# Low parts of the expert weights written over the raw chunk in a one-core MoE decoder step

## What is computed

```python
x = x + mixer(rmsnorm(x))                      # pooling and gating mixer, then w_out
h = rmsnorm(x)
top_w, top_idx = softmax_of_top4(h @ w_router + b_router)       # 32 experts
for each (token, expert) pair, in blocks of up to 128 rows of one expert:
    gu = h[rows] @ w_up[e] + b_up[e]           # w_up[e]: 1024 x 2048
    glu, lin = min(gu[:, :1024], 7), clip(gu[:, 1024:], -7, 7)
    y = (glu * sigmoid(1.702 * glu) * (lin + 1)) @ w_down[e] + b_down[e]    # 1024 x 1024
x = x + sum of the four y of a row, weighted by top_w
x = x + sigmoid(x @ w_ple_gate) * (p @ w_ple_proj)
return rmsnorm(x), and some state rows
```

## Time and profile before

| what | us |
|---|---|
| median of 3 runs | 1451.01 |
| lowest and highest run | 1450.70, 1453.27 |
| the profiled execution's own time | 1450.99 |
| its span in the trace, first to last instruction | 1448.8 |

### The profile page before, as it was taken

How to read it: one execution, slowest core, us unless ns; L and a number is a source line. 1 busy time by engine, 2 the same in 40 slices (tenths; PEclk the granted TensorE clock), 3 DMA queues, 4 the chain that set the end, 5 groups by cost and what they waited for, 6 DMA issues and landing times.

```text
span 1448.8 us, 19378 instructions
## 1 busy us (share of the span) xinstructions
PE 1407.6 (97%) x6542; PEld 1133.9 (78%) x6542; DVE 1231.5 (85%) x994; ACT 928.0 (64%) x632; POOL 210.7 (15%) x130
## 2 busy tenths in 40 slices
PE   6999988999999999999999999999999999999997
PEld 5895456888888888888888888888888888888665
DVE  5732367999999999999999999999999999999885
ACT  4311144777777777777777777777777777777522
POOL 3131000011111111111111111111111111111100
PEclk9999988999999999999999999999999999999999
DMA  7114245999999999999999999999999999999661
GB/s 259 59 62 158 88 163 213 355 375 375 376 372 372 373 372 365 374 361 369 369 372 372 367 370 373 371 369 375 371 380 368 372 376 372 373 371 364 202 239 58
DMA packets 94168, 457.31 MB, mean 316 GB/s; under 512 B 13314, under 2 KB 14894, under 8 KB 60213
## 3 DMA queue, kind: packets, MB, share of 16 engines
q1 hardware_dynamic: 84255, 437.50, 79.6%
q0 software_dynamic: 9360, 17.85, 3.2%
q10 hardware_dynamic: 526, 1.60, 0.4%
HBM read 451.76 MB, written 21.58 MB: 327 GB/s over the span
## 4 chain that ended last, share of the span: by engine, by line
PE 91%; DVE 4%; issue 1%; DMA 1%; ACT 1%; SPq 0%; POOL 0%; POOLq 0%; DVEq 0%; ACTq 0%
PE ps L1257 47%; PE ps L1266 24%; PE ps L1134 5%; PE ps L1404 2%; PE ps L1273 2%; PE ps L1245 2%; PE ps L1238 2%; DVE w_lo L1653 1%; PE ps L1070 1%; PE ps L1072 1%; PE ps L1077 1%; DMA w_v_sb<-in_w_in_dram 1%; DVE resid L1884 1%; PE ps L1149 1%; PE ps L1205 1%
## 5 line engine op out<-in xcount | busy, mean ns | idle before, releaser
L1653 DVE TENSOR_TENSOR w_lo<-raw,w_hi 128x2048 fp32r<-128x2048 f32 x384 | 867.5, 2286 | 60.6 <-PE ps L1266 60.4
L850 ACT ACTIVATE w_hi<-raw 128x2048 fp32r<-128x2048 f32 x384 | 732.4, 1916 | 215.4 <-PE ps L1257 178.0
L1257 PE MATMUL ps<-w_hi,xT_hi 128*128 128x512 f32 x1024 | 278.5, 394 | 0.0
L1266 PE MATMUL ps<-w_lo,xT_hi 128*128 128x512 f32 x1024 | 275.2, 391 | 2.7 <-DVE w_lo L1653 2.6
L1257 PE MATMUL ps<-w_hi,xT_lo 128*128 128x512 f32 x1024 | 276.1, 392 | 0.1
L1266 PEld LDWEIGHTS ps<-w_lo,xT_hi 128*128 128x128 f32 x1024 | 192.5, 188 | 44.1 <-DVE w_lo L1653 4.3
L1257 PEld LDWEIGHTS ps<-w_hi,xT_lo 128*128 128x128 f32 x1024 | 193.2, 189 | 41.9 <-DVE xT_lo L1710 0.5
L1257 PEld LDWEIGHTS ps<-w_hi,xT_hi 128*128 128x128 f32 x1024 | 190.3, 189 | 38.2 <-ACT xT_hi L873 0.2
L702 POOL DMA_INDIRECT expert_rows<-y_rows,scatter_col x32 | 138.1, 4316 | 404.5 <-ACT y_rows L887 404.5
L1257 PE MATMUL ps<-w_hi,aT_hi 128*128 128x512 f32 x512 | 140.0, 395 | 0.0
L1257 PE MATMUL ps<-w_hi,aT_lo 128*128 128x512 f32 x512 | 136.9, 389 | 0.0
(11 more groups left out here) (272 smaller groups left out, 1191.4 us busy)
## 6 DMA issues: line engine op xcount, KB each, us to landing
raw<-in_w_up_dram SPq DMA_DIRECT2D x256, 1024.0 KB, 6.6
raw<-in_w_down_dram SPq DMA_DIRECT2D x128, 1024.0 KB, 7.6
raw<-in_w_ple_gate_dram SPq DMA_DIRECT2D x4, 1024.0 KB, 5.5
yk<-expert_rows SPq DMA_DIRECT2D x4, 1024.0 KB, 8.6
raw<-expert_rows SPq DMA_DIRECT2D x4, 1024.0 KB, 7.9
resid<-in_x_prompt_dram SPq DMA_DIRECT2D x4, 512.0 KB, 10.2
w_v_sb<-in_w_in_dram SPq DMA_DIRECT2D x2, 1024.0 KB, 9.4
w_z_sb<-in_w_in_dram SPq DMA_DIRECT2D x2, 1024.0 KB, 12.7
```

What stands on the lines that cost most here:

```text
L850: act.activation(w_hi[:, s % SPLIT, :], raw[:, s % RING, :], ACT.Copy).then_inc(s_hi, 1)
L1257: mm = pe.matmul(out[:, c:c + 512], (xh, xl)[xs], w_hi[:, s % SPLIT, base + c:base + c + 512], start=(fresh and xs == 0 and base == 0), st ...
L1266: mm = pe.matmul(out[:, c:c + 512], xh, w_lo[:, s % SPLIT, base + c:base + c + 512], start=False, stop=last and k == len(parts) - 1, skip_ ...
L1653: dve.tensor_tensor(w_lo[:, s % SPLIT, :], raw[:, s % RING, :], w_hi[:, s % SPLIT, :].bitcast(F32), ALU.subtract).then_inc(s_lo, 1)
```

## The change

`w_lo` no longer has a buffer of its own: it is laid over `raw`, slot by slot, so the low part of a chunk is written over the raw chunk that it was made from. The three old slots stay allocated as `spare`, so that nothing else moves. VectorE drops its wait for the low products of chunk n - 3. A raw slot is now read last by TensorE's low products, so the loads wait for `s_lused` in place of `s_lo`; that includes the four copies of the gate's weights.

```diff
@@ buffers @@
         with ExitStack() as s:
             raw = sb("raw", [P, RING, 2 * FF], scope=s)
+        with ExitStack() as s:
+            w_lo = sb("w_lo", [P, RING, 2 * FF], F32R, scope=s)
...
-            w_lo = sb("w_lo", [P, SPLIT, 2 * FF], F32R, scope=s)
+            sb("spare", [P, SPLIT, 2 * FF], scope=s)
@@ waits @@
+        def wait_lo_used(eng, J, s):
+            eng.wait_ge(s_lused, STEP_CHUNKS * J + s + 1)
+
@@ sync: raw_free @@
                     if STEP_CHUNKS * J + s >= RING:
-                        wait_lo(sp, J, s - RING)
+                        wait_lo_used(sp, J, s - RING)
                     return
                 lo = sp.to_reg(J * STEP_CHUNKS + (s - RING + 1))
-                sp.wait_ge(s_lo, lo)
+                sp.wait_ge(s_lused, lo)
@@ tensor: lo_products @@
-                        mm = pe.matmul(out[:, c:c + 512], xh, w_lo[:, s % SPLIT, base + c:base + c + 512],
+                        mm = pe.matmul(out[:, c:c + 512], xh, w_lo[:, s % RING, base + c:base + c + 512],
@@ vector: lo_part @@
-                wait_split_used(dve, s_lused, J, s)
                 wait_hi(dve, J, s)
-                dve.tensor_tensor(w_lo[:, s % SPLIT, :], raw[:, s % RING, :], w_hi[:, s % SPLIT, :].bitcast(F32),
+                dve.tensor_tensor(w_lo[:, s % RING, :], raw[:, s % RING, :], w_hi[:, s % SPLIT, :].bitcast(F32),
                                   ALU.subtract).then_inc(s_lo, 1)
```

## The result

The change made the kernel slower by 0.3%: median 1456.68 us of 20 runs (1451.55 to 1459.74), against 1452.20 of 20 runs of the kernel before (1450.37 to 1453.63). The ratio is 1.003, interval 1.0022 to 1.0038. The forecast was 1452.0, and its range ended at 1455.2. A second set, run with the last experiments, gave 1454.46 (12 runs, 1451.90 to 1459.79) against 1452.65, ratio 1.0018 [1.0008, 1.0029]. The loss is some 0.2 to 0.4%, and a run of the changed kernel varies by 8 us where one of before varies by 3 to 4.

A forecast was written before the change was run, and what follows sets the result against it. The prediction took TensorE, busy 97% of the span, to bound the kernel. From 1450.99 us, with 0 for steps, removed wait, in-place writing and start, and +1.0 for the tail, it forecast 1452.0 us, range 1450.3 to 1455.2.

The forecast's parts named there:

- The steady steps: later by 5 us, and it fits: Expert steps: loads issue 5.2 us later, may take 8.52 us to land, worst landing estimated at 7.0; cost 0.
- Raw loads alone no longer queue: Expert steps: releases 2.72 us apart, against 2.50 us for a load's bytes, leave no queue of raw loads.
- Its lead absorbs that: Expert steps: ScalarE's high part starting at 831.2 instead of 830.82 is covered by ScalarE's lead.
- Cost: 0: Expert steps: later loads cost TensorE nothing, hidden by the four chunks it still has to work off.
- the tail: Behind the last expert: gate copy 2 lands later and delays ScalarE's last copy-out; +1.0 us, bounds 0.4 to 2.0.
- writing in place: VectorE's low parts: estimated from line 1902's in-place products at 2.31 us against 2.286, at most 0.4 per step; taken as 0.
- the removed VectorE wait: Expert steps: VectorE's 58.1 us of waiting for TensorE goes, but no product starts earlier; gain 0.
- the start: First ring load, chunk 6: lands at 223.8, its high part 0.4 us late against a lead of 4.2; cost 0.
- shorter median landings (near 5 to 6 us): Raw loads in the expert steps: a sign named in advance for the forecast being right; down loads' median before was 7.6.
- Late loads stall each step: Rival, loads sharing the DMA with the scatter: landings don't shrink, 9 us over 30 steps, so 1461; chance 0.14.
- VectorE freed: Rival, TensorE's gaps at the start: freed of a wait, VectorE removes up to 4.3 us, so 1447.7; chance 0.07.
- Nothing on the path changes: Rival, tail: copy 2 lands in 4.3 us or less, or the late copy-out is caught up; 1451.0, chance 0.17.

The follow-up runs named there:

- product_one_later: The changed kernel, with each load waiting for the low products of one chunk later: 1539.67 us, ratio 1.0575 to the kernel before.
- light scatter: The changed kernel, with the scatter of expert rows cut by its bound to row 0 and those rows filled once early: one execution, 1453.07 us.
- after_copy_out_first: The changed kernel, with the last copy-out moved ahead of the gate's third high part on ScalarE: 1456.78 us, ratio 1.0025 to the kernel before.
- low_part_one_later: The kernel before, own low-part buffer kept, each load waiting for the low part of one chunk later: 1452.21 us, ratio 0.9997.
- before_no_branch: The kernel before, with the branch over the unused overflow blocks left out of TensorE's program: 1452.42 us, ratio 0.9998.
- after_rotated_copy_first: The changed kernel, third down chunk's low products moved to the next step's head and last copy-out put first: 1454.80 us, ratio 1.0012 to the kernel before.

## Why the prediction was wrong

**Failed: "The steady steps: later by 5 us, and it fits".** The allowed 8.52 us fits the runs: with the slowest up load at 8.2 almost no lead is left, and product_one_later, which takes 2.72 from it, stalls at once. The other side was mis-sized. I took the lone landing, added the bytes of gather and scatter at the full rate, and called 7.0 us the worst. It is the median (6.9 and 7.1); the worst are 8.2 and 8.8. The step under it, "Raw loads alone no longer queue", fell: with releases at TensorE's pace, 320 of 351 loads leave with two or more others on their way, and landings stay at 7 us. The step took a spacing of 2.72 us against 2.50 for the bytes as enough, but that works off only 0.2 us of queue with each load. That no step stalled for long is luck in part: the shortest lead left is 0.05 us. I also set aside the DMA share of 0.99 because another stretch moved 420 GB/s. It was the better sign; the light scatter points to one reason, a scatter that costs more than its bytes. The Trainium skill, "DMA: Bandwidth & Descriptors" (Anatomy of one DMA), fits a DMA on the software path as 2.0 us plus the bytes at 436 GB/s, an estimate of 4.4 us for 1 MB. That is further still from what a load of this stream takes on SyncE's hardware queue, 6.9 to 7.1 us.

**Failed: "Its lead absorbs that", with the "Cost: 0" of the steps taken for the last step too.** For 29 steps it nearly does, +1.4 us in the profile, most of it in three steps. But I costed ScalarE's lateness in the steady step only, where TensorE has later work queued. I did not follow VectorE, which stands behind ScalarE, into the last step: there a branch waits behind its low part, and in the profiled execution 1.6 us of lateness became 5.4 us, by a longer branch and the fall of the clock. The row of the branch (5.13 us) and the gap it already left (1.67 us, "issue") were in the trace of before, and I read neither.

**Right in place, half in size: the tail.** +1.0 was forecast, +0.5 measured: the issue came 0.04 us behind its release, not 0.18, and the landing took 5.09, not 5.4. after_copy_out_first shows the mechanism, and that taking it out does not show in the time.

**Right:** writing in place, 0 forecast and 1 ns measured; the removed VectorE wait, worth nothing; the start, 39.95 us before and 40.10 after for the first step; SyncE's and ScalarE's new waits. The sign "shorter median landings (near 5 to 6 us)", which I had named for being right, did not appear. "No low part is written in place now" was wrong, at no cost: `gate_lo` lies over `raw`, and line 1852 writes each of the gate's low parts over its own raw slot. Its rows in the trace of before have the very shape, and show in place what line 1653 takes there into another buffer (median 2283 ns), so the detour over line 1902 was not needed:

```profile
L1852 DVE TENSOR_TENSOR gate_lo<-raw,gate_hi x4: 2273/2283/2286, 1361.7 to 1370.8; 128x2048 fp32r<-128x2048 f32 x4
```

**The rivals.** *Late loads stall each step* had the right premise, that landings do not shrink, and the right sign, but not the right place: the slowest landing was 8.8, the steps nearly held, and the loss came at the exit and in a few steps, and not 30 times. *VectorE freed* did not happen. *Nothing on the path changes* is excluded by the interval.

**What stays open:** how much of the queue in which a load takes 7 us, against 4.7 alone, is the scatter's doing; and what decides from run to run how late chunk 378 is (30.6 to 32.4 us into the last step in the traces of the changed kernel and its variants with the same release), how long the branch's packet takes to start, and whether the clock falls. That these three together make the wide spread is argued from a few traces, not shown.

## What to carry to other kernels

When a slot's release moves behind a later reader, budget the landing that loads have in the running stream, not the lone landing plus bytes: moving the issue by 5 us here left the 7 us unchanged. Then look past the steady step to the iteration behind which no further work is queued, and at any branch there: lateness that the next iteration hides is paid where the pipeline drains, and a fall of the clock can make it dearer. A wait off the path is slack: VectorE's 58 us of waiting for TensorE showed that it ran ahead, and the change turned that into waiting for landings.

## What the runs showed of the hardware

- One taken branch behind a long loop took 3.6 to 6.5 us of TensorE's sequencer: 3.61 in low_part_one_later, 5.13 in the kernel before, 6.45 in product_one_later. In all twelve traces it ended 1.3 to 1.5 us behind one 16 KB packet of an instruction queue, which started 0.95 to 4.02 us into the branch.
- Loads of 1 MB that were issued 2.7 us apart landed 2.5 to 2.6 us apart in the changed kernel, so that a queue shrank by 0.2 us a load and landings stayed near 7 us.
- Whether the clock falls is not told by the length of the gap alone. It fell at the exit behind gaps of 4.27, 4.19, 3.30 and 2.02 us, and did not behind 2.42, 2.37, 1.87 and 1.67.
- In the tail, gains of about 1 us or less did not show in the time three times (before_no_branch, after_copy_out_first, after_rotated_copy_first); in each of their profiles the clock was at the lower level for longer there than in the profile of before. That the one is the reason for the other is not shown.
- GpSimd's scatter instruction was busy for 6.2 us on average in the changed kernel and 4.3 before, for the same rows; the profile's spans on that engine are rough.
